# Numbering a token's six expert rows by loop order, loading part of them before the last pass, and weighing them in pairs

## The reference, cut to what matters

```
scores = sigmoid(x2 @ w_router)                      # 64 experts
_, idx = top_k(scores + router_bias, 6)
gate = take_along_axis(scores, idx); gate = gate / gate.sum(-1) * 2.5
for each expert e and its tokens:
    hb = silu(xb @ w_gate[e]) * (xb @ w_up[e])       # 1024 -> 256
    yb = hb @ w_down[e]                              # 256 -> 1024
    acc[tokens] += yb * gate                         # six weighted rows a token
ffn = acc + (silu(x2 @ w_sh_gate) * (x2 @ w_sh_up)) @ w_sh_down
x = layer_norm(alpha * x + ffn)
```

## Time and profile before

| what | value |
|---|---|
| median of 3 runs | 2006.47 us (2005.06 to 2008.48) |
| profiled execution, its own time | 1997.47 us |
| its span | 1995.7 us |
| PE busy | 1804.0 us (90%) |
| PEld busy | 1112.1 us (56%) |
| DVE busy | 800.1 us (40%) |
| ACT, POOL busy | 381.5 us, 375.5 us |
| loads and stores | 541.75 MB, mean 271 GB/s |
| mean granted TensorE clock | 0.969 |

### The profile page before, as it was taken

The page is one execution under the profiler, slowest core; times in us unless marked ns, Lnnn a source line. Parts: engine busy times, 40 slices in busy tenths (PEclk is TensorE's granted clock), DMA queues, the critical chain, the costliest instruction groups (busy, mean ns, idle before and its releaser), DMA issues. The chain is left out here.

```text
span 1995.7 us, 35283 instructions
## 1 busy us (share of the span) xinstructions
PE 1804.0 (90%) x12176; PEld 1112.1 (56%) x12177; DVE 800.1 (40%) x2156; ACT 381.5 (19%) x874; POOL 375.5 (19%) x499
## 2 busy tenths in 40 slices
PE   9999999889999989879899869999789999997787
PEld 7888445446666545544344428754456666664443
DVE  4222753623333222226276763415523333332236
ACT  2111741001111111101244533211001111110020
POOL 8452000011111111110013752200011111111110
PEclk9999999989999999999899968999899999999999
DMA  6220224599999999997122120107699999999987
GB/s 232 84 70 17 96 113 191 206 401 414 420 420 421 420 421 420 421 416 296 58 70 74 41 53 3 54 33 283 279 419 394 424 421 423 421 423 423 423 364 295
DMA packets 144053, 541.75 MB, mean 271 GB/s; under 512 B 30902, under 2 KB 68370, under 8 KB 94174
## 3 DMA queue, kind: packets, MB, share of 16 engines
q1 hardware_dynamic: 122654, 490.20, 61.3%
q0 software_dynamic: 21312, 50.37, 6.5%
HBM read 521.58 MB, written 46.14 MB: 284 GB/s over the span
## 5 line engine op out<-in xcount | busy, mean ns | idle before, releaser
L669 PE MATMUL bank<-W,XT 128*64 128x256 f32 x2880 | 335.5, 390 | 43.0 <-DMA W<-in_w_exp_gate_dram 15.8
L669 PEld LDWEIGHTS bank<-W,XT 128*64 128x64 f32 x2880 | 235.6, 141 | 154.7 <-issue 39.9
L704 PE MATMUL bank<-W,ht 128*64 128x512 f32 x720 | 168.0, 608 | 13.8 <-DMA W<-in_w_exp_down_dram 8.3
L2113 PE MATMUL bank<-XT,room 128*128 128x512 f32 x352 | 157.7, 603 | 0.0
L680 DVE TENSOR_TENSOR sig<-sig,bank 128x256 f32<-128x256 f32 x72 | 30.3, 421 | 274.7 <-ACT sig L676 264.4
L722 POOL DMA_INDIRECT y_rows<-y,row x36 | 36.7, 1020 | 430.6 <-DVE y L715 430.6
L682 DVE TENSOR_TENSOR h<-sig,bank 128x256 f32<-128x256 f32 x72 | 30.4, 422 | 209.9 <-PE bank L669 209.8
L2113 PEld LDWEIGHTS bank<-XT,room 128*128 128x128 f32 x352 | 66.8, 193 | 84.5 <-issue 84.1
L722 POOL DMA_INDIRECT y_rows<-XT,row x36 | 36.4, 1010 | 407.1 <-DVE XT L715 407.1
L655 ACT ACTIVATE XT<-bank 128x512 f32<-128x512 f32 x74 | 44.2, 597 | 330.5 <-PE bank L647 330.5
L669 PE MATMUL bank<-room,XT 128*64 128x256 f32 x864 | 98.7, 380 | 8.5 <-DMA room<-in_w_exp_gate_dram 8.0
(11 more groups left out here) (457 smaller groups left out, 2746.8 us busy)
## 6 DMA issues: line engine op xcount, KB each, us to landing
W<-in_w_exp_gate_dram SPq DMA_DIRECT2D x88, 1024.0 KB
W<-in_w_exp_up_dram SPq DMA_DIRECT2D x88, 1024.0 KB
W<-in_w_exp_down_dram SPq DMA_DIRECT2D x88, 1024.0 KB
room<-in_w_exp_gate_dram SPq DMA_DIRECT2D x40, 1024.0 KB
third_high<-in_w_exp_up_dram SPq DMA_DIRECT2D x40, 1024.0 KB
third_high<-in_w_exp_down_dram SPq DMA_DIRECT2D x40, 1024.0 KB
W<-y_rows SPq DMA_DIRECT2D x8, 2048.0 KB, 14.2
room<-in_rwkv_w_in_dram SPq DMA_DIRECT2D x22, 512.0 KB
```

The source lines that it names most:

```text
L669: last = pe.matmul((gate, up)[m][64 * a:64 * a + 64, :], xt[s][:, k, 64 * a:64 * a + 64], weights(w, a, m)[:, k * FE:(k + 1) * FE], start= ...
L704: last = pe.matmul(B[5 + half][64 * a:64 * a + 64, :], ht[:, j, 64 * a:64 * a + 64], weights(w, a, 2)[:, at:at + 512], start=(j == 0), sto ...
L2113: last = pe.matmul(main(i)[:], wc[i % WBUFS][:, kb, :], K.XT[:, kb, :], start=(kb == 0), stop=(kb == KD - 1))
```

## The change

1. **Row numbers.** `slot_cols` no longer holds the top-k place of an expert but how many of the token's experts the loop takes up to it: a running sum over the mask (L483 of the changed kernel) and four operations (L486) in the place of one. So a token's rows 0 to 5 are written in the order of the passes. The gates must then be put in that order: 12 more DVE instructions a layer after the gates are made, from `seen` to `picked` (L532 to L545). The plan's small products go to bank 5, since bank 4 is read later than before.
2. **Loads.** SP waits in `load` on the scatters' own semaphores, first only for the passes through the last but one pair. Of a token's six rows, at most two belong to the last pair, so rows 0 to 3 are then in HBM. It issues rows 0 to 3 of tiles 0 and 1 (4 MB), then waits for all scatters and issues the rest (8 MB). Rows (2q, 2q+1) of a tile are a pair q.
3. **Form of the loads.** Pair 0 of tiles 0 and 1 (`BY_VECTOR`) is loaded as before, a token a partition. The other ten pairs are loaded stacked: row 2q of 64 tokens on partitions 0 to 63 and row 2q+1 of the same tokens on partitions 64 to 127, by two transfers of 64 partitions and 512 KB each.
4. **Weighing.** A diagonal is now 128 x 64, two 64 x 64 diagonals one above the other, so that one product of 64 stationary columns adds both rows of 64 tokens. For that the gates are turned once in pass 0 (`turn_gates` on PE, `keep_gates` on ACT). PE weighs ten pairs, four products each, where it had 32 products, and DVE weighs two pairs in all (4 instructions of L959's kind, before 8), ahead of its sums by tile.

```diff
-BY_VECTOR = 2
-BY_TENSOR = TOPK - BY_VECTOR
+ROW_PAIRS = TOPK // 2
+HP = P // 2
+BY_VECTOR = ((0, 0), (1, 0))
+BY_TENSOR = [(t, q) for t in range(NT) for q in range(ROW_PAIRS) if (t, q) not in BY_VECTOR]
...
-                    last = pe.matmul(B[4][0:1, q * P:(q + 1) * P], plan[:, q:q + 1], ident[:], start=True, stop=True)
+                    last = pe.matmul(B[5][0:1, q * P:(q + 1) * P], plan[:, q:q + 1], ident[:], start=True, stop=True)
...
+                flat = mask[:].rearrange("p t e -> p (t e)")
+                step(dve.tensor_tensor_scan(seen[:].rearrange("p t e -> p (t e)"), flat, flat, 0.0, ALU.add, ALU.bypass))
                 with nc.allow_low_precision(reason="multiples of 512 up to 2560 are exact in bfloat16"):
-                    step.inc(dve.tensor_scalar(K.slot_cols[:, :, :, 2:4], at.rearrange("p t (i a) -> p t i a", a=2), float(T), -float(T), ALU.mult, ALU.add))
+                    for t in range(NT):
+                        step.inc(dve.tensor_scalar(K.slot_cols[:, t, :, 2:4], seen[:, t, :].rearrange("p (i a) -> p i a", a=2),
+                                                   float(T), -float(T * (TOPK * t + 1)), ALU.mult, ALU.add))
...
+                step(dve.scalar_tensor_tensor(seen[:], K.iota_e[:].unsqueeze(1).to_broadcast([P, NT, E]), -float(E), mask[:], ALU.add, ALU.mult))
+                step(dve.scalar_tensor_tensor(seen[:], seen[:], -8.0, at, ALU.mult, ALU.add))
+                for t in range(NT):
+                    step.inc(dve.max(ordered[:, t, :], seen[:, t, :]))
+                dve.wait_ge(steps, step.n)
+                step(dve.tensor_scalar(whole[:], ordered[:], 0.125, -0.4375, ALU.mult, ALU.add))
+                step(dve.tensor_scalar(whole[:], whole[:], float(2 ** 23), -float(2 ** 23), ALU.add, ALU.add))
+                step(dve.scalar_tensor_tensor(which[:].rearrange("p (t j) -> p t j", t=NT), whole[:, :, 0:TOPK], -8.0,
+                                              ordered[:, :, 0:TOPK], ALU.mult, ALU.add))
+                step(dve.tensor_tensor(picked[:], which[:].unsqueeze(2).to_broadcast([P, NT * TOPK, TOPK]),
+                                       K.iota_j[:].unsqueeze(1).to_broadcast([P, NT * TOPK, TOPK]), ALU.is_equal))
+                by_tile = picked[:].rearrange("p (t i) j -> p t i j", t=NT)
+                step(dve.tensor_tensor(by_tile, by_tile, K.gates[:].unsqueeze(2).to_broadcast([P, NT, TOPK, TOPK]), ALU.mult))
+                step(dve.tensor_reduce(K.gates[:].rearrange("p t j -> p (t j)"), picked[:], AX.X, ALU.add))
...
+            if isinstance(n, int) and n == 1:
+                pe.wait_ge(ending.gates_kept, 1)
...
+        def turn_gates(pe):
+            for h in range(2):
+                for j in range(2):
+                    last = pe.matmul(gates_bank[HP * j:HP * j + HP, h], ident[:, HP * h:HP * h + HP],
+                                     K.gates[:, :, j:TOPK:2], start=True, stop=True)
+            last.then_inc(gates_turned, 1)
+
+        def keep_gates(act):
+            act.wait_ge(gates_turned, 1)
+            act.activation(turned_gates[:], gates_bank, ACT.Copy).then_inc(ending.gates_kept, 1)
...
-                ending.load(sp)
+                before_last = passes_through(PAIRS - 2)
+                turns = sp.value_load(K.plan_turns[0:1, 0:1], min_val=PAIRS // 2, max_val=MAX_PASSES // 2)
+                ending.load(sp, [held(sp, ((before_last + 1) >> 1) << 4), held(sp, (before_last >> 1) << 4)],
+                            held(sp, turns * 16))
...
-                pool.memset(tok_f[0][:], 0.0).then_inc(ending.y_stored, 1)
...
+                        turn_gates(pe)
...
+                    if isinstance(n, int) and n == 0:
+                        keep_gates(act)
...
-        self.rows = K.arena.rearrange("p (t j d) -> p t j d", t=NT, j=TOPK)
+        self.rows = K.arena.rearrange("p (t q h d) -> p t q h d", t=NT, q=ROW_PAIRS, h=2)
+        self.y_half = K.y_rows.rearrange("(j t h p) d -> t j p h d", j=TOPK, t=NT, h=2)
+        self.diagonal = room[:, 0, 0:2 * len(BY_TENSOR) * HP].rearrange("p (n h q) -> p n h q", h=2, q=HP)
+        self.two = room[:, 0, KD * FE - HP:KD * FE]
...
+    def load_pair(self, sp, t, q):
+        if (t, q) in BY_VECTOR:
+            sp.dma_start(self.rows[:, t, q], self.y[t][:, 2 * q:2 * q + 2]).then_inc(self.loaded[t][q], 16)
+            return
+        for j in range(2):
+            sp.dma_start(self.rows[HP * j:HP * j + HP, t, q], self.y_half[t][2 * q + j]).then_inc(self.loaded[t][q], 16)
...
+    def load(self, sp, early, every):
         K, ln = self.K, self.ln
-        sp.wait_ge(self.y_stored, 1)
-        for t in range(NT):
-            sp.dma_start(self.rows[:, t, BY_VECTOR:TOPK], self.y[t][:, BY_VECTOR:TOPK]).then_inc(self.loaded_t[t], 16)
-            sp.dma_start(self.rows[:, t, 0:BY_VECTOR], self.y[t][:, 0:BY_VECTOR]).then_inc(self.loaded_v[t], 16)
+        for s in range(2):
+            sp.wait_ge(self.stored[s], 16)
+            sp.wait_ge(self.stored[s], early[s])
+        for t in range(2):
+            for q in range(ROW_PAIRS - 1):
+                self.load_pair(sp, t, q)
+        for s in range(2):
+            sp.wait_ge(self.stored[s], 16)
+            sp.wait_ge(self.stored[s], every)
+        for t, q in ((0, 2), (1, 2), (2, 0), (2, 1), (2, 2), (3, 0), (3, 1), (3, 2)):
+            self.load_pair(sp, t, q)
...
+    def row_product(self, pe, t, q):
+        B, n = self.K.banks, BY_TENSOR.index((t, q))
+        pe.wait_ge(self.diagonals, 2 * n + 2)
+        pe.wait_ge(self.loaded[t][q], 32)
+        for half in range(2):
+            for h in range(2):
+                last = pe.matmul(B[2 * t + half][HP * h:HP * h + HP, :], self.diagonal[:, n, h, :],
+                                 self.rows[:, t, q, h, half * 512:(half + 1) * 512],
+                                 start=False, stop=(q == ROW_PAIRS - 1))
+            if q == ROW_PAIRS - 1:
+                last.then_inc(self.summed, 1)
...
+        self.shared_product(pe, 0)
+        self.row_product(pe, 0, 1)
+        self.shared_product(pe, 1)
+        self.row_product(pe, 1, 1)
+        pe.wait_ge(self.scaled, 1)
+        self.row_product(pe, 0, 2)
+        self.row_product(pe, 1, 2)
+        self.shared_product(pe, 2)
+        self.row_product(pe, 2, 0)
+        self.row_product(pe, 2, 1)
+        self.row_product(pe, 2, 2)
+        self.shared_product(pe, 3)
+        self.turn(pe, 0)
+        for q in range(ROW_PAIRS):
+            self.row_product(pe, 3, q)
+        for t in range(1, NT):
+            self.turn(pe, t)
...
+        for t, q in BY_VECTOR:
+            dve.wait_ge(self.loaded[t][q], 16)
+            dve.wait_ge(self.scaled, t + 1)
+            for j in range(2):
+                step(dve.scalar_tensor_tensor(X[:, t, :], self.rows[:, t, q, j, :], K.gates[:, t, 2 * q + j:2 * q + j + 1],
+                                              X[:, t, :], ALU.mult, ALU.add))
...
-        for t in range(NT):
-            for j in range(BY_TENSOR):
-                act.activation(self.diagonal[:, t, j, :], K.ident[:], ACT.Copy,
-                               scale=K.gates[:, t, BY_VECTOR + j:BY_VECTOR + j + 1]).then_inc(self.diagonals, 1)
+        for j in range(2):
+            half = slice(HP * j, HP * j + HP)
+            act.activation(self.two[half, :], K.ident[half, half], ACT.Copy).then_inc(self.two_made, 1)
+        act.wait_ge(self.gates_kept, 1)
+        act.wait_ge(self.two_made, 2)
+        for n, (t, q) in enumerate(BY_TENSOR):
+            for h in range(2):
+                act.activation(self.diagonal[:, n, h, :], self.two, ACT.Copy,
+                               scale=self.gates[:, h, t, q:q + 1]).then_inc(self.diagonals, 1)
```

More of the change, by code:

```diff
@@ L332, in routed_experts_tables @@
         end = sb("end", [P, PAIRS])
+        seen = sb("seen", [P, NT, E])
+        ordered = sb("ordered", [P, NT, 8])
+        whole = sb("whole", [P, NT, 8])
+        which = sb("which", [P, NT * TOPK])
+        picked = sb("picked", [P, NT * TOPK, TOPK])
         turn = sb("turn", [P, MAX_PASSES // 2])
@@ L562, in expert_loop @@
         third = [[K.room[:, 0, :], K.room[:, 1, :]], [high[:, 0, :], high[:, 1, :]], [high[:, 2, :], high[:, 3, :]]]
-        ending = Combination(K, L, scope, shared, out, next_weights, high)
+        stored = [sem("stored0"), sem("stored1")]
+        ending = Combination(K, L, scope, shared, out, next_weights, high, turned_gates, stored)
         slots = B[4][:, 0:4]
+        gates_bank = B[3][:, 0:2 * NT * ROW_PAIRS].rearrange("p (h t q) -> p h t q", h=2, t=NT)
         gate, up = B[2][:, 0:FE], B[7][:, 0:FE]
@@ new lines, in shared_product @@
+    def shared_product(self, pe, t):
+        B, shared = self.K.banks, self.shared
+        for half in range(2):
+            for j in range(2):
+                pe.matmul(B[2 * t + half][:], shared.hidden[:, j, t * P:(t + 1) * P], shared.w[:, j, half * 512:(half + 1) * 512],
+                          start=(j == 0), stop=False)
```

(20 more changed lines are left out.)

43 lines of the change are left out of this document (10 added, 33 removed).

## The result

| | before | changed |
|---|---|---|
| median | 2005.76 us (4 runs, 1999.5 to 2008.48) | 2042.2 us (4 runs, 2040.99 to 2044.07) |
| span of the profiled execution | 1995.7 us | 2040.1 us |
| mean granted TensorE clock | 0.969 | 0.960 |

The ratio is 1.0192, 95% interval 1.0175 to 1.0208: 36 us slower (a reading of the medians), where 16.7 were forecast, and above the top of the forecast's range, 2037. The direction was right, the size less than half of the measured one. The two traces differ by 44.4 us. Some 8 us of that are not the change: the trace of before is of an execution 8.3 us under that kernel's median, the other is of one at its median.

What follows compares the result with a forecast made beforehand. Expert loops are bound by weight transfers at about 420 GB/s, so end delays shift everything. Tables and pass 0 +2.8, layer 1's ending +4.0, layer 0's +9.9 sum to 16.7 us; 2006.47 + 16.7 = 2023 us, range 1997 to 2037.

Steps and rivals of the forecast that it cites:

- Tables and pass 0: Both layers' tables 2.4 us later, gate turning in pass 0 costing 0.4 in layer 0, nothing in layer 1: +2.8 us.
- Weighing on PE: Endings: PE's products for a stacked pair take 1.8 us; 3.6 if the column halves do not overlap.
- Loads on 64 partitions: Endings: half-partition row loads move at 250 GB/s, so a pair takes 4.2 us against 2.6 at full rate.
- the 270 beside it: GB/s in the before trace for two 192 KB half loads on opposite halves, issued 0.6 us apart.
- The bound of 204: Lower bound in GB/s for half-partition loads, half of 408; a pair then takes 5.1 us.
- Ending of layer 1: Layer 1 from first row loads to its end: 1995.4 against 1991.4, +4.0 us.
- the early part: Layer 1's ending: left weights 2.4 us, two full-width pairs 5.2, two stacked 8.4; from 1936.4 to 1952.4.
- The late part: Layer 1's rows after the last scatter: eight stacked pairs 33.6 us, two output stores 2.6, done at 1988.8.
- Ending of layer 0: Layer 0: rows issued at 906.5 behind next weights, pairs take 47.2 us, end 961.7 against 951.74: +9.9 us.
- Strictly half the rate: Rival, chance 0.15: half loads in both endings get 204 GB/s, 5.1 us a pair; 2041 us.
- Full rate: Rival, chance 0.26: halves fill each other's gaps, PE paces both endings; 10.0 us faster, 1996 us.
- The early load is not early: Endings: early load gains little at any rate, 0.9 us in layer 0, about 4 MB in layer 1; no separate chance.

Runs made afterwards that it cites:

- tables_only: The kernel before with only the changed kernel's row numbering and gate reordering: 2007.15 us, ratio 1.0021.
- experiment 10: Gate turning moved behind the last pass: in the changed kernel 2044.3 us; in a kernel with aligned slots and full-width stacked loads in layer 1 only, 1994.38 us.
- experiment 1: The changed kernel with row loads on 128 partitions, same number, size and order, stacking left out (sums weigh wrong rows): 2005.28 us, ratio 1.0002.
- experiment 2: The changed kernel without the early load, the first four pairs waiting for every scatter: 2045.06 us, ratio 1.0218.
- experiment 5: The changed kernel with the upper half of each stacked pair issued from ScalarE's queue, the lower from SyncE: 2034.21 us, ratio 1.0158.
- experiments 8 and 11: Kernel before with 96 unused bytes in front of third_high: 2005.43 us, 1.0008; kernel before with all weight slots at multiples of 256 bytes: 1997.61 us, 0.9968.

## Why the prediction was right or wrong

By the medians 19.7 us are missing (36.4 against 16.7), by the traces 27.7 (44.4 against 16.7). The account below is by the traces.

*Tables and pass 0, +2.8.* Right as far as the times can tell. tables_only measured +2.8 for the tables alone, against 2.4, with a wide interval, and the wait in front of `shared_hidden(1)` is gone as said. The trace of the changed kernel has 4.7. "In layer 1 I count nothing" for the turning may have missed the step of 3.6 us at the fourth pass (experiment 10), whose cause and worth in time stayed open.

*Weighing on PE, 1.8 us a pair.* Right: 1.94 at full clock, up to 3.68 where the clock had fallen in a wait (920.58; 0.50 granted from 916 to 920.5, with PE busy for 0.00 us). The prediction took 3.6 as a sign that its step on PE is wrong; it is not, since the same products take 1.94 at 1.00.

*Loads on 64 partitions, 250 GB/s.* This is the step that failed. While only half loads flow the rate is 222 to 226 in both endings, and a pair takes 4.65 us and not 4.2: 4.5 us for layer 0's ten pairs. The lone load's 229 was the true figure. What pulled me up was the 270 beside it, a window of 1.25 us; against 40 us at 222 it says nothing on how halves run together. The bound of 204 was too low as well.

*Ending of layer 1, +4.0; measured +16.9.* Here most is missing, and in the second step that failed: the early part, which I put at 16 us. It ended 13.8 us late. From the first row issue (1962.75) to the last early pair (1993.7) the core moved 7.3 million bytes in 31 us, 236 GB/s. I had counted 5.2. Of the 2.1 that I had not, 0.6 are the last scatter (0.39; it landed after 12.3 us and not 8.3) and more left weights than I took: 1.2 for 0.98 (in the trace of before 1.6 flow from 1935.35 to 1946, 0.39 of them the scatter). The other 1.5 are rows of the late part, which flow before the last early ones are in. At 236 GB/s my 5.2 are 22.0 us (+6.0), the 0.6 are 2.7 and the 1.5 are 6.4, and the first row flowed 1.1 us sooner than I had it: 14.0.

Half of the 7.3, that is left weights, scatter and two pairs of full width (3.7 million bytes), has nothing to do with half loads. Had it gone at 408 and the rest at 226, the stretch would be 25 us and not 31. So the mixture as a whole was slower than both prices make it (131 GB/s from 1968 to 1970). That is not how full-width pairs fare everywhere: in layer 0, without left weights and a scatter beside them, the rate is 406 in 920 to 922. What makes the mixture slow stays open. My error was to price its parts one by one.

*The late part,* 35.0 us against 36.2, looks right and is luck. As long as only half loads flow a pair takes 4.6 (five of them from 1993.82 to 2016.95), so that eight would be 37.2 and with two stores 39.8. The 1.5 million bytes that had come before made up for that. From the last landing to the end it was 7.1 against 6.65.

*Ending of layer 0, +9.9; measured +18.3.* Of the 8.4 missing, 4.5 are the rate. 1.5 are the issue: it came at 910.45 (908.0 without the later loop) and not at 906.5, for 2.0 us pass on SP between the end of its last small weight's issue (908.46) and the first row's. About 2 are the end of the transfers, where the rate falls before the last pair is in (152 GB/s from 963 to 964, 29 from 964 to 965), which I had not counted. 0.3 are the tail.

*The rivals.* Strictly half the rate (0.15) gave 2041 and came out within 1 us of 2042.2, by luck: its pair of 5.1 us is too dear by 0.45, and its early part nearly as short as mine. Full rate (0.26) is refuted as a rate; its time of 1996 was not reached at full width either (2005.28), in part for the clock (experiment 1). "The early load is not early" was right (experiment 2). The Trainium skill, SBUF — State Buffer, section Door 1: The DMA port swizzle, gives 218 GB/s for 64 partitions, and the trace's 222 to 226 agrees with it better than with my 250; the estimate made from it, 2035, is 7 us too low, since it had the same early part as mine.

## What to carry to other kernels

Price a transfer by the partitions it reaches: with 64 of them queued by one engine, the rate here was 55% of that with 128 (226 of 408). A full-width transfer in the same queue can still have its own rate (406), but where weights, a scatter and both forms were in flight together, everything came at 236. So price such a stretch by all its bytes, and not by its parts. When data must land on two halves, lay them out in DRAM so that one transfer brings both. And look at where a tile that takes in transfers begins: 96 bytes in front of it made a loop bound by transfers 1.5 us longer in the traces, and aligning all weight slots was worth 6.6 us by the medians, where the new ending on top of that brought 5.2, with intervals that overlap.

## What the runs showed that I had not expected

- The last scatter of layer 1 lands 3.4 us after its issue with nothing beside it, 7.6 beside rows on 128 partitions (experiment 1) and 12.3 beside rows on 64 (changed kernel). It did not lengthen the ending: without the early load it lands after 3.2 us, and layer 1 ends at the same point (experiment 2).
- Two issuing engines move opposite halves at 294 to 314 GB/s, one engine at 226 (experiment 5).
- Packets of 8 KB take 309 ns, each of them, where all weight slots begin at a multiple of 256 bytes, and 313 on the mean where none does (experiments 8 and 11); packets of 4 KB 159.0 and 160.4. The Trainium skill, DMA: Bandwidth & Descriptors, section How a descriptor splits into AXI transactions, has pieces that must begin at multiples of 256 bytes, with one more for a start in between. By that, 33 pieces for 32 would be an estimated 3%. The mean packet shows 1.2%, for a third or more of them took 309 ns all along.
- A stall that PE and the transfers share is 3 us longer in the traces of kernels that do 0.4 us of work more several passes earlier. Moving that work took 2.9 us off it in one kernel and 1.0 in another (experiment 10), so the cause is not settled.
